# Attention on one core: the meta keys' weights of two query tiles turned in one transposition, their products read 16 rows each

## The reference, cut to what matters

```
s = einsum(q_nope, k_nope) + einsum(q_rope, k_rope)      # queries x 2064 keys
s = where(key_chunk <= query_chunk, s * scale, -1e30)    # meta keys: chunk 0, frames: 1 + t // 64
p = softmax(s)                                           # over the keys
o = p @ v                                                # 64 values a head
out = (o * silu(z)) @ w_o
```

## Time and profile before

| | us |
|---|---|
| median of 3 runs | 2631.14 |
| lowest, highest | 2626.5, 2634.41 |
| the profiled execution, time | 2619.49 |
| the profiled execution, span | 2617.7 |
| attention stage, about | 575 to 1573 |

### The profile page before, as it was taken

One profiled execution on the slowest core, in us unless ns is written; L12 is line 12 of the kernel. 1 busy time (PEld: TensorE's weight loads), 2 busy tenths in 40 slices (PEclk: granted clock), 3 DMA queues, 4 the chain that ended last, 5 costly groups with the idle time before them and its releaser, 6 DMA issues. The chain is left out here.

```text
span 2617.7 us, 48053 instructions
## 1 busy us (share of the span) xinstructions
PE 2554.9 (98%) x17333; PEld 2405.0 (92%) x17333; DVE 1889.0 (72%) x3883; ACT 1450.1 (55%) x3540; POOL 436.5 (17%) x206
## 2 busy tenths in 40 slices
PE   6999999999999999999999999999999999999998
PEld 6899999999999999999999996888999999999787
DVE  5546661129998889898898985788888666666766
ACT  4434322238888888888888881225445445444210
POOL 1000000012454445444444410000000000000000
PEclk8999999999999999999999999999999999999999
DMA  4655454312233434333333316765554543553443
GB/s 156 196 164 190 146 164 123 112 44 51 51 82 83 95 81 97 83 74 80 81 75 90 75 47 181 215 191 176 207 181 171 197 154 129 183 190 137 142 144 112
DMA packets 245281, 337.06 MB, mean 129 GB/s; under 512 B 86386, under 2 KB 182530, under 8 KB 232514
## 3 DMA queue, kind: packets, MB, share of 16 engines
q1 hardware_dynamic: 227218, 325.61, 41.5%
q10 hardware_dynamic: 17840, 8.52, 1.1%
HBM read 224.54 MB, written 108.98 MB: 127 GB/s over the span
## 5 line engine op out<-in xcount | busy, mean ns | idle before, releaser
L1248 DVE TENSOR_TENSOR b_pt_lo<-b_transposed,b_pt_hi 128x384 fp32r<-128x384 f32 (+4 forms) x784 | 429.1, 564 | 49.7 <-ACT b_pt_hi L1141 46.2
L1141 ACT ACTIVATE b_pt_hi<-b_transposed 128x384 fp32r<-128x384 f32 (+4 forms) x784 | 382.3, 502 | 117.3 <-PE b_transposed L1175 108.2
L1128 ACT ACTIVATE ground<-b_ring,ground 128x384 f32<-128x384 f32 (+7 forms) x784 | 436.3, 561 | 19.6 <-DVE ground L1238 11.6
L1233 DVE TENSOR_REDUCE ground<-b_ring 128x1 f32<-128x384 f32 (+7 forms) x784 | 409.7, 528 | 27.6 <-PE b_ring L45 14.8
L1175 PE MATMUL b_transposed<-identity,ground 128*128 128x128 f32 (+2 forms) x2448 | 380.0, 272 | 8.0 <-DVE b_pt_lo L1248 5.0
L1175 PEld LDWEIGHTS b_transposed<-identity,ground 128*128 128x128 f32 (+2 forms) x2448 | 279.8, 134 | 55.7 <-issue 25.4
L43 PE MATMUL b_ring<-region 128*128 128x384 f32 (+7 forms) x784 | 301.2, 384 | 4.1 <-DVE b_transposed L1209 2.4
L43 PE MATMUL p_banks<-p_x_hi,big 128*128 128x258 f32 x896 | 254.3, 284 | 10.2 <-DVE big L581 8.8
L45 PE MATMUL b_ring<-region 128*128 128x384 f32 (+7 forms) x784 | 258.7, 330 | 0.0
L44 PE MATMUL b_ring<-region 128*128 128x384 f32 (+7 forms) x784 | 258.5, 330 | 0.0
L45 PE MATMUL p_banks<-p_x_hi,big 128*128 128x258 f32 x896 | 254.1, 284 | 0.0
(11 more groups left out here) (213 smaller groups left out, 6408.1 us busy)
## 6 DMA issues: line engine op xcount, KB each, us to landing
ground<-x_a SPq DMA_DIRECT2D x23, 1032.0 KB, 5.6
ground<-w_conv SPq DMA_DIRECT2D x32, 512.0 KB, 3.7
c_tiles<-w_conv SPq DMA_DIRECT2D x32, 512.0 KB, 3.9
c_ln<-weight_sums SPq DMA_DIRECT2D x16, 1024.0 KB, 8.0
c_tiles<-weight_sums SPq DMA_DIRECT2D x16, 1024.0 KB, 7.2
weight_sums<-c_tiles SPq DMA_DIRECT2D x9, 1024.0 KB, 3.9
keys<-ground SPq DMA_DIRECT2D x64, 129.0 KB, 5.2
queries<-ground SPq DMA_DIRECT2D x64, 129.0 KB, 2.6
```

What stands on the lines that cost most here:

```text
L1128: nc.scalar.activation(p[0:rows, n % PSLOTS, 0:w], banks[0:rows, n % RING, 0:w], ACT.Exp, bias=nmax[0:rows, tile % 8:tile % 8 + 1], accum_ ...
L1141: nc.scalar.activation(turned(pt_hi, g, u, nb)[:, :, tile_columns(u, j)], tb[:, n % 2, 0:nb, 0:rows], ACT.Copy).then_inc(pt_hi_done, 1)
L1233: ins = nc.vector.tensor_reduce(top, bank[0:rows, 0:w], AX, ALU.max, negate=(chunks == 1))
L1248: nc.vector.tensor_tensor(lo, tb[:, n % 2, 0:nb, 0:rows], hi.bitcast(F32), ALU.subtract).then_inc(pt_split, 1)
```

## The change

- The even tile's meta block is no longer transposed. DVE copies the even tile's first 32 exponentials into the first 32 columns of the odd tile's slot of `p` (`copy_meta`, one copy a unit, 128 x 32). The odd tile's exponentials of chunk 0 begin at column 32 (`META_COPIED`, `tile_first`). One transposition of 48 columns turns both: the even tile's meta keys come to rows 0 to 15, the odd tile's to rows 32 to 47.
- H and L of the even tile's chunk 0 copy one block less (`turned_blocks`, `turned_tile`).
- The values of the meta keys stand twice in `v`, in rows 0 to 15 and in rows 32 to 47 (POOL copies them for each head, DVE for the first).
- In P of chunk 0 the meta product of 256 (272) columns becomes two of 128 columns with operands of 16 rows: the even tile's from rows 0 to 15, as second product of the high and of the low pass; the odd tile's from rows 32 to 47, both at the end of P, behind a wait (`first_added`) for the even tile's low one. In unit 0 the meta queries' 16 columns are a product of their own, of 16 rows, ahead of the even tile's.
- T of the odd tile waits for the copy (`meta_copied`), as does the E that overwrites the even tile's slot.

```diff
+def turned_blocks(u, j, x):
+    blocks = tile_blocks(u, j, x)
+    return blocks[1:] if x == 0 and j != META_TILE and j % 2 == 0 else blocks
...
+META_COPIED = 32
+COPIES = [(SCORE_AT[h, u, 2 * u, 0], SCORE_AT[h, u, 2 * u + 1, 0]) for h in range(HEADS) for u in range(UNITS)]
+COPIES_AT = {max(TURNED_AT[odd] - 3, 0): n for n, (even, odd) in enumerate(COPIES)}
+COPY_OF = {even: n for n, (even, odd) in enumerate(COPIES)}
+def tile_first(j, x):
+    return META_COPIED if x == 0 and j != META_TILE and j % 2 else 0
...
+                nc.gpsimd.tensor_tensor(v[META_COPIED:META_COPIED + META, h % 2, 0, :], v[0:META, h % 2, 0, :].bitcast(F32), zero[0:META, 0:1].to_broadcast([META, 2 * VH]), ALU.add).then_inc(v_repeated, 1)
+                pool.wait_ge(v_repeated, h)
...
+                    if n - PSLOTS in COPY_OF:
+                        act.wait_ge(meta_copied, COPY_OF[n - PSLOTS] + 1)
+                    at = tile_first(j, x)
-                    nc.scalar.activation(p[0:rows, n % PSLOTS, 0:w], banks[0:rows, n % RING, 0:w], ACT.Exp,
+                    nc.scalar.activation(p[0:rows, n % PSLOTS, at:at + w], banks[0:rows, n % RING, 0:w], ACT.Exp,
...
-                    for c, (_, keys, _) in enumerate(tile_blocks(u, j, x)):
-                        last = nc.tensor.transpose(tb[0:keys, n % 2, c, 0:rows], p[0:rows, s % PSLOTS, col:col + keys], ident[0:rows, 0:rows])
+                    blocks = turned_blocks(u, j, x)
+                    col = META * (len(tile_blocks(u, j, x)) - len(blocks)) + tile_first(j, x)
+                    for c, (_, keys, vb) in enumerate(blocks):
+                        if vb == 0 and j != META_TILE:
+                            pe.wait_ge(meta_copied, UNITS * h + u + 1)
+                            last = nc.tensor.transpose(tb[0:META_COPIED + META, n % 2, c, 0:rows], p[:, s % PSLOTS, 0:META_COPIED + META], ident[:, :])
+                        else:
+                            last = nc.tensor.transpose(tb[0:keys, n % 2, c, 0:rows], p[0:rows, s % PSLOTS, col:col + keys], ident[0:rows, 0:rows])
...
+                    meta = blocks[0][2] == 0
+                    order = [1, 0] + list(range(2, len(blocks))) if meta else range(len(blocks))
+                    def meta_product(pt, i, stop=False):
+                        rows = slice(META_COPIED * i, META_COPIED * i + META)
+                        return nc.tensor.matmul(ob[:, P * i:P * i + P], v[rows, h % 2, 0, :], turned(pt, n, u, len(blocks))[rows, 0, P:2 * P], start=False, stop=stop)
+                    def products(pt, high):
+                        for c in order:
+                            if blocks[c][2]:
+                                part = slice(P if n in UNIT_ENDS and c == len(blocks) - 1 else 0, 2 * P)
+                                last = nc.tensor.matmul(ob[:, part], v[:, h % 2, blocks[c][2], :], turned(pt, n, u, len(blocks))[:, c, part],
+                                                        start=(high and x == 0 and c == int(meta)), stop=(not high and not meta and n in UNIT_ENDS and c == len(blocks) - 1))
+                                continue
+                            if u == 0:
+                                cols = tile_columns(u, META_TILE)
+                                nc.tensor.matmul(ob[:, cols], v[0:META, h % 2, 0, :], turned(pt, n, u, len(blocks))[0:META, 0, cols], start=False, stop=False)
+                            first = meta_product(pt, 0)
+                            if not high:
+                                first.then_inc(first_added, 1)
+                        return last
...
+                    products(pt_hi, True)
                     pe.wait_ge(pt_split, LAST_TURNED[n] + 1)
+                    last = products(pt_lo, False)
+                    if meta:
+                        pe.wait_ge(first_added, UNITS * h + u + 1)
+                        meta_product(pt_hi, 1)
+                        last = meta_product(pt_lo, 1, n in UNIT_ENDS)
...
+            def copy_meta(k):
+                even, odd = COPIES[k]
+                dve.wait_ge(exps, even + 1)
...
+                if odd >= PSLOTS:
+                    dve.wait_ge(t_done, TURNED_AT[odd - PSLOTS] + 1)
+                nc.vector.tensor_copy(p[:, odd % PSLOTS, 0:META_COPIED], p[:, even % PSLOTS, 0:META_COPIED]).then_inc(meta_copied, 1)
...
                 elif letter == "L":
+                    if n in COPIES_AT:
+                        copy_meta(COPIES_AT[n])
```

More of the change, by code:

```diff
@@ L909, in stage_b @@
         first_hi, first_split, hi_done = sem("b_first_hi"), sem("b_first_split"), sem("b_hi_done")
+        v_repeated, meta_copied, first_added = sem("b_v_repeated"), sem("b_meta_copied"), sem("b_first_added")
         keys_loaded = lambda h: 64 * (h - 1) + 16
@@ L930, in turned, with turned_tile @@
             return pt[:, g % 2, 0:blocks * w].rearrange("p (c q) -> p c q", q=w)
+        def turned_tile(pt, g, u, j, x):
+            first = len(tile_blocks(u, j, x)) - len(turned_blocks(u, j, x))
+            return turned(pt, g, u, len(tile_blocks(u, j, x)))[:, first:, tile_columns(u, j)]
         raw_gate = raw[:, :].rearrange("p (a t) -> p a t", t=GATE)
@@ L949, in next_values @@
                 if h == 0:
-                    sp.wait_ge(first_split, 2)
+                    sp.wait_ge(first_split, 3)
                 elif h <= WO_PIECES:
@@ L1096, in split_weights @@
                 pool.wait_ge(wo_split, k + 1)
-            pool.wait_ge(first_split, 2)
+            pool.wait_ge(first_split, 3)
             for h in range(HEADS):
@@ L1136, in _ @@
                     _, u, j, x = SCORES[s]
-                    nb, rows = len(tile_blocks(u, j, x)), tile_tokens(j)[1]
+                    nb, rows = len(turned_blocks(u, j, x)), tile_tokens(j)[1]
                     act.wait_ge(t_done, n + 1)
@@ L1140, in _ @@
                         act.wait_ge(pv_done, g - 1)
-                    nc.scalar.activation(turned(pt_hi, g, u, nb)[:, :, tile_columns(u, j)], tb[:, n % 2, 0:nb, 0:rows], ACT.Copy).then_inc(pt_hi_done, 1)
+                    nc.scalar.activation(turned_tile(pt_hi, g, u, j, x), tb[:, n % 2, 0:nb, 0:rows], ACT.Copy).then_inc(pt_hi_done, 1)
                 else:
@@ L1167, in _ @@
                     s, _ = TURNED[n]
-                    _, u, j, x = SCORES[s]
+                    h, u, j, x = SCORES[s]
                     rows = tile_tokens(j)[1]
@@ L1181, in _ @@
                         if h == 0:
-                            pe.wait_ge(first_split, 2)
+                            pe.wait_ge(first_split, 3)
                         else:
@@ L1187, in _ @@
                     blocks = blocks_of(u, x)
-                    part_of = lambda c: slice(P if n in UNIT_ENDS and c == len(blocks) - 1 else 0,
-                                              2 * P + META if blocks[c][1] == META and u == 0 else 2 * P)
+                    meta = blocks[0][2] == 0
[3 more added lines that the diff above has]
+                        return nc.tensor.matmul(ob[:, P * i:P * i + P], v[rows, h % 2, 0, :], turned(pt, n, u, len(blocks))[rows, 0, P:2 * P], start=False, stop=stop)
@@ L1190, in _ @@
                     pe.wait_ge(pt_hi_done, LAST_TURNED[n] + 1)
-                    for c, (k0, keys, vb) in enumerate(blocks):
-                        nc.tensor.matmul(ob[:, part_of(c)], v[:, h % 2, vb, :], turned(pt_hi, n, u, len(blocks))[:, c, part_of(c)],
-                                         start=(x == 0 and c == 0), stop=False)
+                    products(pt_hi, True)
                     pe.wait_ge(pt_split, LAST_TURNED[n] + 1)
-                    for c, (k0, keys, vb) in enumerate(blocks):
-                        last = nc.tensor.matmul(ob[:, part_of(c)], v[:, h % 2, vb, :], turned(pt_lo, n, u, len(blocks))[:, c, part_of(c)],
-                                                start=False, stop=(n in UNIT_ENDS and c == len(blocks) - 1))
+                    last = products(pt_lo, False)
@@ L1212, in _ @@
             nc.vector.tensor_tensor(v[0:META, 0, 0, VH:], raw_v_blocks[0:META, 0], v[0:META, 0, 0, 0:VH].bitcast(F32), ALU.subtract).then_inc(first_split, 1)
+            dve.wait_ge(first_split, 2)
+            nc.vector.tensor_copy(v[META_COPIED:META_COPIED + META, 0, 0, :], v[0:META, 0, 0, :].bitcast(F32)).then_inc(first_split, 1)
             def inverse_sums(h):
@@ L1220, in inverse_sums @@
                 nc.vector.reciprocal(r_sb[:, h % 2, :], r_sb[:, h % 2, :]).then_inc(r_done, 1)
+            def copy_meta(k):
+                even, odd = COPIES[k]
+                dve.wait_ge(exps, even + 1)
+                if FIRST_STAGED <= odd < PSLOTS:
+                    for s in range(STAGE):
+                        dve.wait_ge(stored[s], STORED[s])
+                if odd >= PSLOTS:
+                    dve.wait_ge(t_done, TURNED_AT[odd - PSLOTS] + 1)
+                nc.vector.tensor_copy(p[:, odd % PSLOTS, 0:META_COPIED], p[:, even % PSLOTS, 0:META_COPIED]).then_inc(meta_copied, 1)
             for letter, n in VECTOR_STEPS:
```

(4 more changed lines are left out.)

1 line of the change is left out of this document (removed).

## The result

| | us | against before |
|---|---|---|
| before, median of 4 | 2628.95 | |
| changed, median of 4 | 2830.88 (2822.49 to 2843.32) | 1.0771 [1.0737, 1.0806] |
| the profiled execution, changed: time, span | 2834.29, 2832.4 | |

The change costs about 203 us (194 to 212), where 112 were forecast, with 155 as the high end.

What follows compares the result with a forecast made beforehand. PE was taken to bound attention (988 of 998 us): +122 us on PE less 12 of waits caught up is +110 on 2619.5, 2729.5; with the profiled execution 11.6 below the median, 2741 us, range 2700 to 2784.

Steps and rivals of the forecast that it cites:

- the high end: Top of the forecast range, 2784 us: 2631 + 148 from the high bound on PE, plus 5 for the median's scatter.
- PE as the bound, pitch as price: Attention stage: PE busy 988 of 998 us, so each PE instruction costs its pitch, 0.12 us a product, 0.11 a transposition.
- the transposition's 0.11: Per unit, the even tile's meta transposition goes, -0.11 us; the odd tile's wider one costs nothing.
- the count of visits and products: Three 16-row visits per unit, one in each pass and one at the end; 512 + 32 narrow products replace 256 wide.
- PE empties at a 16-row operand: At each 16-row visit PE empties: 0.21 us in, 0.11 to 0.16 out, then 0.11 for a bare full load.
- The size of a visit: On PE: +0.29 us for a visit in a pass, +0.47 for that at the end; +0.94 a unit, 120 us.
- my high bounds: Narrow loads at a wide load's 0.11 pitch: +0.34 us a visit in a pass, +0.57 at the end; 146 us.
- the page that I set aside: Skill page on LDWEIGHTS: a 32-row load lasts as long as a 128-row one; by it the sum nears the high bound.
- Waits caught up, 12 us: PE's idle time before transposition loads, 35 + 18 us, partly caught up by longer turns: 12 us, from 0 to 30.
- first_added and meta_copied at nothing: Both new semaphore waits cost 0: a 128-row product covers the first; the copy's Exp is long done for the second.
- The step that failed: the copy: DVE's new 128 x 32 copy: 0.11 us by the 64 x 64 memset, 14 us (0 to 20), leaving DVE even.
- DVE as the bound, 0.01: Rival: DVE bounds attention through the copy; 894 - 17 + 14 stays under PE's 988 + 110; chance 0.01.

Runs made afterwards that it cites:

- e9_reduce_copy: Changed kernel with DVE's copy at the same place made by a TENSOR_REDUCE (maximum over an axis of one) instead of COPY; 2763.26 us, 1.0515.
- e4_before_narrow: Kernel before with only its meta products in both passes reading 16 rows instead of 128, meta queries' columns a separate product; 2715.35 us, 1.0342.
- e3_wide_act: Changed kernel with all meta products reading 128 rows instead of 16 (output differs) and the copy made by ACT; 2650.78 us, 1.0095.
- e7_one_visit: Changed kernel with the copy on ACT and all 16-row products in one visit at the end of P instead of three; 2705.12 us, 1.0322.
- e1_act_copy: Changed kernel with the copy of the even tile's 32 exponentials made by ACT instead of DVE, at the same turn; 2761.13 us, 1.0514.
- e10_before_reduce: Kernel before with the copy alone added, as a TENSOR_REDUCE on DVE into columns nobody reads; 2636.38 us, 1.0041.

## Why the prediction was wrong, point by point

- **PE as the bound, pitch as price; the transposition's 0.11; the count of visits and products.** Right as long as no copy is held: in e9_reduce_copy PE is idle for 12 of 1141 us.
- **PE empties at a 16-row operand.** Right, by e4_before_narrow, e3_wide_act and e7_one_visit. The way in is 0.21 as forecast (in the high pass 0.29 where it was 0.20, the same loss).
- **The size of a visit.** Mis-sized. I took the narrow load at 0.062 from the earlier trace rows, and 0.29 and 0.47 us a visit; measured are 0.108, 0.33 and 0.56, my high bounds (0.34, 0.57). The sum is 2 x 0.33 + 0.56 - 0.11 = 1.11 us a unit, 142 us, and 3.5 us for the meta queries' products, where I had 122. Why the loads of the earlier trace rows were quicker isn't shown: they were f32 transpositions with 16 columns to follow, these are fp32r products with 128. For this term the page that I set aside was right: by the Trainium skill, TensorE: Matmul & The Clock Gate, LDWEIGHTS, rows don't shorten a load. By that page the sum was the high bound, 148, and the rows of the changed kernel give 146.
- **Waits caught up, 12 us.** The net is right in size: 146 on PE's stream became 135 in e1_act_copy. That may be luck. The forecast had the copy's own length as covered, yet e10_before_reduce puts a copy that is never held at 11 us on the kernel before, and e3_wide_act stands at +25 where 12 were expected. How much was caught up and how much the copy took wasn't separated.
- **first_added and meta_copied at nothing.** first_added was right, by reason of the product between, as e7_one_visit shows. meta_copied was right in its order: DVE's idle time before all 128 copies is 0.3 us, so none waits for its Exp. It was not right in effect, by the next point.
- **The step that failed: the copy.** I priced it at 0.11 us by the nearest row, the 64 x 64 memset of the earlier trace rows, bounded it at 0.16 and called it covered. On its own it is 0.18; as COPY beside POOL its mean is 0.82 and its longest 4.31. The holds cost 67 us of the 203 (e9_reduce_copy against the changed kernel), of which the forecast had nothing; without them the change costs 135 us, inside the range. The nearest row for its length was no row for its form: every DVE group of the sum either touches PSUM or is a reduction, and none is a COPY between SBUF tiles while POOL works. The earlier trace rows had POOL busy for 428 of 998 us, and I counted POOL only for its own new instruction.
  The rule stands in the Trainium skill, GPSIMD Engine Reference, Specifications: DVE and GpSimd share their SBUF interfaces, with contention for DVE instructions in a 2-port mode; and by VectorE: DVE Perf Modes, Mode 2x_2P, a tensor_copy from SBUF to SBUF can run in one even in fp32. The runs agree: the COPY is held (mean 0.82 us for 0.18) and the reduction isn't (at most 0.189). In them the hold lasts until POOL's running instruction has ended.
- **DVE as the bound, 0.01.** It was looked for in DVE's sum of busy time. It came instead as single holds of up to 4.3 us in front of L, against which a share of 90% says nothing.
- **Together:** 110 of my sum stands beside 135 measured for the change without holds, and the holds add 67. The high end, +155, holds the 135 but not the 203.

## What to carry to other kernels

A 16-row matmul among 128-row ones cost PE's emptying here, on the way in and on the way out, and not its own time. Padding its operand with zeros, as the kernel before does, avoids that; gathering such products in one visit makes it less (+85 us for +135). A wide product ahead of each wait on their own results would hide that wait too, as in the changed kernel; the two together were not tested. An instruction that is added to an engine is priced by a row of the same form between the same memories, and by what runs beside it on the other engines. Here the longest instruction of POOL (4.6 us) was the bound for one copy of DVE (4.3 us), and the copy stood ahead of L, for which PE, the bound, waits.

## What the runs showed of the hardware that was not expected

- A DVE COPY of 128 x 32 from SBUF to SBUF (0.18 us) that is held ends 0.034 to 0.046 us after the end of the POOL TENSOR_TENSOR that it meets (the changed kernel, 41 of 128) and lasts up to 4.31 us; a TENSOR_REDUCE over an axis of one with the same data runs through in 0.173 to 0.189, an ACT copy in 0.22 to 0.26.
- A load of 16 rows x 128 columns for fp32r products has a pitch of 0.108 us, as one of 128 rows; the f32 one of the earlier trace rows had 0.062.
- A wait of PE for its own matmul with nothing between costs 0.27 us (e7_one_visit).
- After an idle time of 3.81 us the granted clock of the 10 us around it was 0.72.
